# A hybrid state-space and delta-rule decoder layer on one core: prologue scalars and input products moved, the small projection in slots of its own, and the end of the kernel rebuilt with tokens turned before the last norm and six stores

## The chip, the cores and the metric

The kernel runs on one core of a Trainium2 chip. The metric is the device time of one execution in microseconds (us). The kernel before took 2083.59 us, the median of three runs (2082.62 to 2084.09). Engines: PE is TensorE, DVE is VectorE, ACT is ScalarE, POOL is GpSimd, SP is the engine that issues nearly all transfers.

## The reference, cut to what matters

One decoder layer for 320 tokens (256 of a prompt, 8 x 8 of samples) of width 2048, all in float32:

```
h = RMSNorm(x);  proj = h @ w_in -> u | qkv | z | beta | a | gate_s5 | gate_dn
A: S5 state-space model: lambda = exp(a*dt), B' = ((lambda-1)/a) * B, scan over positions, y = Re(C h) + D u
B: gated DeltaNet: beta = sigmoid(.), g = -exp(a_log)*softplus(a + dt_bias), conv + SiLU on q, k, v, chunked delta rule
x = x + (sigmoid(gate_s5)*(A @ w_a) + sigmoid(gate_dn)*(B @ w_b)) @ w_out
x = x + (silu(h2 @ w_gate) * (h2 @ w_up)) @ w_down;  x = x + (p @ w_ple) * sigmoid(h3 @ w_ple_gate)
y = RMSNorm(x) * g_final
```

## The kernel before, in words

Activations lie with features on the partitions: a tile [128, 16, 320] holds x. Weights stream through a ring of four "units"; a unit is 512 KB, four blocks of 128 rows by 256 columns. For every unit SP loads `raw`, ACT copies it to a rounded `whi` (`split_hi`, L909), DVE subtracts to get `wlo` (`split_lo`, L1345), and PE does 24 matmuls of 320 columns (L2035: high times high, high times low, low times high, for two column halves). Units make pairs (four units for a depth of 2048), whose results lie in `pg`, two sets of PSUM banks used in turn, evacuated by DVE.

Small work is laid between the units by an order written out by hand: `schedule()` gives a list of slots, each a list of side jobs and a number of units. PE does a slot's side jobs and then its units. ACT and DVE do the units of a slot (their split) first and then its side jobs. Side jobs of PE write two other PSUM areas, side_a and side_b, whose fills follow the list of `side_fills()`. Each engine runs its instructions in order, so what waits holds up all behind it.

The prologue. Tokens are turned into xt0 (`x`, L2042), weighted by g into xhi and xlo (`x+`). `s5a` computes the S5 scalars on 32 partitions (DVE L1436 to L1448), `s5b` goes on with two Sin on ACT and sixteen DVE instructions (L1456 to L1471). `s5par` turns them (PE L2111) to the layout sp5, `h0` and `cst` turn states (PE L2118, L2095), `rows` squares each token row for the first norm (ACT L1008), `norm` 0 gives the inverse roots. `bmix` multiplies B by the scalars (`b_discrete`, DVE L1486 to L1491, six instructions for each of two factors) and spreads it (L1496), `bb` and `ct` turn B and C (PE L2127, L2148), `k0` multiplies them (L2139), `cadv` advances C by lambda (DVE L1516 to L1522, twice). `ba` is the small projection for beta and a: PE L2159, a copy by DVE (L1618), a turn (`bat`, PE L2165), and then softplus and sigmoid of the decays, with ACT and DVE answering each other (DVE L1630, L1631; ACT L1057, L1059, L1060; DVE L1633, L1634). POOL builds tables of powers of lambda (`tables`) once s5par is there. Then come sixteen s5 slots, a tail, eight `conv` slots of two units each (DVE L1667: nine multiply-adds per head; ACT: `silu_head` and `first_taps`), and the delta rule, output, feed-forward (two halves) and per-layer-embedding parts, the last three in loops.

`pt` turns the embedding input p (PE L2042 on ptok) between the first and the second pair of the first half's down projection; DVE waits there for it and copies it to pf (L1932).

The end. The last pair's gate goes through ACT's sigmoid, DVE multiplies (L1969) and adds to xt (L1972, one instruction for both 128-row blocks), ACT squares (L917) and weights into xg (L1301), POOL adds the squares to acc (L878, L880), PE sums them over partitions (`norm(3)`, L2059), ACT computes the inverse root by Ln and Exp (L935, L942), PE turns xg back to tokens in six fills of eight transposes (`fin`, L2463), ACT and DVE scale each fill into yo (L1331, L2010) and SP stores y in three transfers (L626). yo holds two blocks of tokens, so the third waits for the first store to land.

Of the kernel before, what the change touches and what calls it, by code (L numbers as in the profile page):

```python
# [17 lines left out]
BF16 = mybir.dt.bfloat16  # L18
# [4 lines left out]
P = 128  # L23
# [64 lines left out]
def side_fills():  # L88
# [28 lines left out]
    order += [("ba"[i % 2], ("emb", i)) for i in range(1, KD // 2)] + [("b", ("norm", 3))]  # L117
    order += [("ab"[j % 2], ("fin", j)) for j in range(6)]
# [18 lines left out]
def schedule():  # L137
# [17 lines left out]
    slot([("x", 2), ("x", 3), ("x+", 2), ("x+", 3)], 1)  # L155
# [12 lines left out]
    slot([("pads",)], 1)  # L168
# [5 lines left out]
    for h in range(H):  # L174
        slot([("conv", h)], 2)
# [57 lines left out]
def hybrid_layer(nc, x_prompt, x_sample, state_conv, state_delta, state_s5_re, state_s5_im, p_prompt, p_sample,  # L233
# [25 lines left out]
    with ExitStack() as ctx:  # L259
# [98 lines left out]
        sqj = Zone(nc, ct_end - 5120, 4096).take("sqj", [P, D], BF16)  # L358
# [81 lines left out]
        yo = zo.take("yo", [P, 2, D])  # L440
        xg = zo.take("xg", [P, KD, N])
# [62 lines left out]
        def _(sp):  # L504
# [116 lines left out]
            for t in range(3):  # L621
                dst, n = [(y_prompt[0, 0:P], P), (y_prompt[0, P:2 * P], P),
                          (y_sample.rearrange("b l d -> (b l) d"), NSM)][t]
                for f in (2 * t, 2 * t + 1):
                    wait_drained(sp, ("fin", f))
                sp.dma_start(dst, yo[0:n, t % 2, :]).then_inc(sem(f"y_stored_{t % 2}"), 16)  # L626
            sp.wait_ge(sem("y_stored_0"), 32)
            sp.wait_ge(sem("y_stored_1"), 16)
# [6 lines left out]
        def _(pool):  # L635
# [261 lines left out]
            add_loop(24, 32)  # L897
# [3 lines left out]
        def _(act):  # L901
# [25 lines left out]
            def root(n):  # L927
# [3 lines left out]
                if n == 0:  # L931
                    o.step(act.activation(invt[:, 0:2], ss[:, 0:2], ACT.Ln, scale=1.0 / D, bias=cst[:, 0:1]))
                    o.step(act.activation(invt[0:NSM, 2:3], ss[0:NSM, 2:3], ACT.Ln, scale=1.0 / D, bias=cst[0:NSM, 0:1]))
                elif n == 3:
                    o.step(act.activation(invt[:, 0:2], ps(key)[:, 1, 0:2], ACT.Ln, scale=1.0 / D, bias=cst[:, 0:1]))  # L935
                    drain(act.activation(invt[0:NSM, 2:3], ps(key)[0:NSM, 1, 2:3], ACT.Ln, scale=1.0 / D, bias=cst[0:NSM, 0:1]), key)
                if n < 3:
                    drain(act.activation(inv[:], ps(key)[:, 0, 0:N], ACT.Ln, scale=1.0 / D, bias=cst[:, 0:1]), key)
                wait_drained(act, key)
                o.settle()  # L940
                if n in (0, 3):
                    o.step(act.activation(invt[:, 0:2], invt[:, 0:2], ACT.Exp, scale=-0.5))  # L942
                    act.activation(invt[0:NSM, 2:3], invt[0:NSM, 2:3], ACT.Exp, scale=-0.5).then_inc(sem("invt_ready"), 1)
                if n < 3:
                    act.activation(inv[:], inv[:], ACT.Exp, scale=-0.5).then_inc(sem("inv_ready"), 1)
# [41 lines left out]
            def side(key):  # L987
# [65 lines left out]
                elif what == "ba":  # L1053
# [243 lines left out]
            def final_x(i):  # L1297
                act.wait_ge(sem("xf_ready"), i + 1)
                finish(xt, i + 24, i, None)
# [25 lines left out]
            for t in range(3):  # L1325
                n = CHUNKS[t][1]
                key = ("fin", 2 * t)
                wait_filled(act, key)
                if t == 2:
                    act.wait_ge(sem("y_stored_0"), 16)  # L1330
                drain(act.activation(yo[0:n, t % 2, 0:D // 2].rearrange("p (k c) -> p k c", k=2), ps(key)[0:n], ACT.Copy,  # L1331
                                     scale=invt[0:n, t:t + 1]), key)
# [3 lines left out]
        def _(dve):  # L1336
# [136 lines left out]
            def b_discrete(j):  # L1473

                dve.wait_ge(sem("bnat_landed"), 32)
# [17 lines left out]
                def spread(src, j):  # L1493
                    for r in range(2):
# [999 lines left out]
```

## Time and profile before

| what | value |
|---|---|
| median of three runs | 2083.59 us (2082.62 to 2084.09) |
| profiled execution, its own time | 2082.91 us |
| its span, first to last instruction | 2081.2 us |
| busy: PE, DVE, ACT, POOL | 98%, 54%, 40%, 14% |
| mean granted TensorE clock | 0.990 of full |

The profile is of one execution. A row of the timeline gives the start, the duration, the engine, the line, the operation, its tiles and shapes, and how often it is repeated; a bracket at its end gives the engine's idle time before it and who ended that. A row of the chain of waits gives the start, the duration and what was on the path. Neighbouring PE rows overlap by up to 0.16 us, because matmuls are pipelined.

### The profile page before, as it was taken

How to read it: one execution, taken by the hardware profiler on the slowest of the kernel's cores; microseconds unless marked ns; L12 is line 12 of the kernel's file. 1: busy time of each engine (PE TensorE's matmuls, PEld its weight loads, DVE VectorE, ACT ScalarE, POOL GpSimd, SP SyncE). 2: the span in 40 equal slices, each digit the busy share in tenths (PEclk: the TensorE clock that was granted, in tenths of full speed). 3: DMA queues.
4: the chain of work that ended last, by engine and by line, in shares of the span. 5: the costliest groups of instructions: out<-in, count | busy, mean ns of one | idle time of the engine just before them, and what ended most of it. 6: DMA issues, size and time to landing. Idle time of an engine off the chain costs nothing.

```text
span 2081.2 us, 38416 instructions
## 1 busy us (share of the span) xinstructions
PE 2031.5 (98%) x15445; PEld 1985.8 (95%) x15445; DVE 1125.2 (54%) x1376; ACT 825.7 (40%) x1075; POOL 289.2 (14%) x370
## 2 busy tenths in 40 slices
PE   8899999999999999999999999999999999999997
PEld 7799999988999979999999999999999999999997
DVE  3899896754544477654444444333444444444553
ACT  5343335762323345244433333223333333334543
POOL 2845542000001110011000000000000000011111
PEclk8999999999999999999999999999999999999999
DMA  6544444543334667754444444444544444444442
GB/s 168 162 143 142 131 122 139 154 118 105 96 112 137 176 192 236 235 184 150 152 145 149 151 151 153 131 152 148 158 147 148 151 151 148 140 151 156 143 147 86
DMA packets 299271, 310.13 MB, mean 149 GB/s; under 512 B 24722, under 2 KB 290019, under 8 KB 298531
## 3 DMA queue, kind: packets, MB, share of 16 engines
q1 hardware_dynamic: 295476, 296.76, 46.6%
q0 software_dynamic: 3264, 11.64, 2.1%
q8 instruction: 83, 1.36, 0.3%
q14 instruction: 30, 0.25, 0.0%
q10 hardware_dynamic: 418, 0.12, 0.0%
HBM read 291.34 MB, written 17.14 MB: 148 GB/s over the span
## 4 chain that ended last, share of the span: by engine, by line
PE 88%; DVE 7%; ACT 2%; issue 2%; DMA 1%; SPq 0%; DVEq 0%; ACTq 0%
PE pg L2035 80%; DVE wlo L1345 2%; DVE cacc L1667 2%; PE side_a L2075 1%; PE side_a L2066 1%; ACT whi L909 1%; PE side_b L2075 1%; DMA raw<-in_w_out 0%; PE side_a L2035 0%; PE side_a L2337 0%; DMA xtok<-in_x_sample 0%; PE side_a L2356 0%; PE side_b L2298 0%; PE side_b L2035 0%; PE side_a L2314 0%
## 5 line engine op out<-in xcount | busy, mean ns | idle before, releaser
L1345 DVE TENSOR_TENSOR wlo<-raw,whi 128x1024 fp32r<-128x1024 f32 (+1 forms) x528 | 650.1, 1239 | 699.0 <-ACT whi L909 697.3
L909 ACT ACTIVATE whi<-raw 128x1024 fp32r<-128x1024 f32 (+1 forms) x528 | 544.8, 1039 | 910.7 <-PE pg L2035 872.2
L2035 PE MATMUL pg<-xhi,whi 128*128 128x320 f32 x2816 | 882.8, 313 | 15.9 <-DVE wlo L1345 15.6
L2035 PE MATMUL pg<-xlo,whi 128*128 128x320 f32 x2816 | 872.5, 310 | 0.0
L2035 PE MATMUL pg<-xhi,wlo 128*128 128x320 f32 x2816 | 872.5, 310 | 0.0
L2035 PEld LDWEIGHTS pg<-xhi,whi 128*128 128x128 f32 x2816 | 531.1, 189 | 25.1 <-issue 13.7
L2035 PEld LDWEIGHTS pg<-xlo,whi 128*128 128x128 f32 x2816 | 531.4, 189 | 0.8
L2035 PEld LDWEIGHTS pg<-xhi,wlo 128*128 128x128 f32 x2816 | 531.0, 189 | 0.0
L2035 PE MATMUL pg<-mhi,whi 128*128 128x320 f32 x704 | 217.4, 309 | 2.5 <-DVE wlo L1345 2.5
L2035 PE MATMUL pg<-mlo,whi 128*128 128x320 f32 x704 | 217.4, 309 | 0.0
L2035 PE MATMUL pg<-mhi,wlo 128*128 128x320 f32 x704 | 217.4, 309 | 0.0
L893 POOL TENSOR_TENSOR fsi<-fsg,inv 128x640 f32<-128x640 f32 x22 | 43.4, 1971 | 710.0 <-ACT fsg L1240 710.0
L2035 PEld LDWEIGHTS pg<-mhi,whi 128*128 128x128 f32 x704 | 132.2, 188 | 2.6 <-issue 2.6
L2035 PEld LDWEIGHTS pg<-mhi,wlo 128*128 128x128 f32 x704 | 132.2, 188 | 0.0
L2035 PEld LDWEIGHTS pg<-mlo,whi 128*128 128x128 f32 x704 | 132.2, 188 | 0.0
L639 POOL TENSOR_TENSOR pt<-ta,tb 128x256 f32<-128x256 f32 x64 | 72.5, 1151 | 99.7 <-DVE gg L1568 98.4
L878 POOL TENSOR_TENSOR acc<-acc,sq 128x320 f32<-128x320 f32 x24 | 24.2, 1007 | 411.6 <-ACT sq L917 411.6
L2035 PE MATMUL pg<-mxhi,whi 128*128 128x320 f32 x256 | 79.2, 309 | 0.4 <-DVE wlo L1345 0.4
L2035 PE MATMUL pg<-mxlo,whi 128*128 128x320 f32 x256 | 79.1, 309 | 0.0
L2035 PE MATMUL pg<-mxhi,wlo 128*128 128x320 f32 x256 | 78.7, 308 | 0.0
L2035 PEld LDWEIGHTS pg<-mxhi,whi 128*128 128x128 f32 x256 | 48.1, 188 | 0.6 <-issue 0.6
L2035 PEld LDWEIGHTS pg<-mxlo,whi 128*128 128x128 f32 x256 | 48.0, 188 | 0.0
(460 smaller groups left out, 1954.1 us busy)
## 6 DMA issues: line engine op xcount, KB each, us to landing
raw<-in_w_in SPq DMA_DIRECT2D x144, 512.0 KB, 3.8
raw<-in_w_gate SPq DMA_DIRECT2D x88, 512.0 KB, 3.5
raw<-in_w_up SPq DMA_DIRECT2D x88, 512.0 KB, 3.5
raw<-in_w_down SPq DMA_DIRECT2D x80, 512.0 KB, 3.5
raw<-in_w_out SPq DMA_DIRECT2D x32, 512.0 KB, 3.5
raw<-in_w_ple_gate SPq DMA_DIRECT2D x32, 512.0 KB, 3.5
raw<-in_w_a SPq DMA_DIRECT2D x16, 512.0 KB, 5.4
raw<-in_w_b SPq DMA_DIRECT2D x16, 512.0 KB, 4.3
```

What stands on the lines that cost most here:

```text
L639: ins = pool.tensor_tensor(out, a, b, op)
L878: pool.tensor_tensor(acc[:], acc[:], sq[:, 0, :], ALU.add).then_inc(sem("pool_steps"), 1)
L893: pool.tensor_tensor(fsi[:], fsg[:], inv[:].unsqueeze(1).broadcast_to([P, 2, N]), ALU.mult).then_inc(sem("fsi_ready"), 1)
L909: act.activation(whi[:, r, 0:nk, :], raw[:, r, 0:nk, :], ACT.Copy).then_inc(w_hi, 1)
L1345: dve.tensor_tensor(wlo[:, r, 0:nk, :], raw[:, r, 0:nk, :], whi[:, r, 0:nk, :].bitcast(F32), ALU.subtract).then_inc(w_lo, 1)
L1667: ins = dve.scalar_tensor_tensor(out=s, in0=qkv[:, t, j:j + NCV], scalar=w, in1=s, op0=ALU.mult, op1=ALU.add)
L2035: ins = pe.matmul(out[:, m, 0:N], w, a, start=first and k == 0 and part == 0, stop=last and k == nk - 1 and part == 2)
L2066: ins = pe.matmul(out[0:rows or P, h // 4, (h % 4) * n:(h % 4) * n + n], lhs(h), rhs(h), start=True, stop=True)
L2075: ins = pe.matmul(out[r, h // 4, (h % 4) * HB:(h % 4 + 1) * HB], lhs(h, r), rhs(h, r), start=True, stop=True)
```

## The change

- `slots`: `s5a` and `s5b` stand one slot earlier and ahead of the x jobs; the products of `bmix` are a job `bprod` of their own, in the slots of rows 0 (factor 1) and rows 1 (factor 0); `bmix` keeps the spread, both in one slot; `cadv` 0 has a slot to itself; `bat` is split from `ba` and stands in the slot of `pads`; the decays (`decay` 0 and 1) move to the conv slots of heads 4 and 5. The number of units in all these slots together is unchanged.
- The squares' scratch sqj lies elsewhere, since the products now use its old place.
- `pt` moves from the first half's down projection to behind the first gate pair of the second half.
- The last squares (block pair 7): DVE's addition to xt is cut in two, ACT squares each, and DVE adds each to acc (POOL did). A square root with a reciprocal on DVE takes the place of Ln and Exp; a tiny Sqrt stands ahead of the last squares.
- `fin`: the first halves of tokens 0 to 127 and 128 to 255 are turned ahead of norm(3), the second into pg; the other two are turned after it; the samples' two halves are made by sixteen matmuls into 128 partitions and scaled by one instruction into their own tile yo2. Six stores of half the columns replace three.

```diff
-    slot([("x", 4), ("x", 5), ("x+", 4), ("x+", 5), ("s5a",)], 1)
-    slot([("x", 6), ("x", 7), ("x+", 6), ("x+", 7), ("s5b",)], 1)
-    slot([("s5par",), ("h0",), ("cst",), ("rows", 0)], 1)
-    slot([("rows", 1)], 1)
+    slot([("s5a",), ("x", 2), ("x", 3), ("x+", 2), ("x+", 3)], 1)
+    slot([("s5b",), ("x", 4), ("x", 5), ("x+", 4), ("x+", 5)], 1)
+    slot([("x", 6), ("x", 7), ("x+", 6), ("x+", 7)], 1)
+    slot([("s5par",), ("h0",), ("cst",), ("rows", 0), ("bprod", 1)], 1)
+    slot([("rows", 1), ("bprod", 0)], 1)
...
-    slot([("bmix", 1)], 2)
-    slot([("bmix", 0)], 1)
+    slot([("bmix", 1), ("bmix", 0)], 2)
     slot([("bb", 1), ("ct",)], 1)
-    slot([("bb", 0), ("k0",), ("cadv", 0)], 1)
+    slot([("bb", 0), ("k0",)], 1)
+    slot([("cadv", 0)], 1)
     slot([("cadv", 1)], 1)
     slot([("ba",)], 1)
-    slot([("pads",)], 1)
+    slot([("bat",), ("pads",)], 1)
...
-        slot([("conv", h)], 2)
+        slot([("conv", h)] + [("decay", h - 4)] * (4 <= h < 6), 2)
...
-                elif what == "ba":
+                elif what == "decay" and a[0] == 0:
                     act.wait_ge(sem("gab_landed"), 32)
                     o.step(act.activation(gab[:, 0:H], gab[:, 0:H], ACT.Exp))
                     act.wait_ge(sem("ba_vector"), 1)
...
+                if c == 1:
+                    wait_filled(dve, ("pt",))
+                    drain(dve.tensor_copy(pf[:], ps(("pt",))[:, :, 0:N]), ("pt",))
+                    wait_drained(dve, ("pt",))
...
+            o.step(act.activation(dl[:, 0:1], cst[:, 0:1], ACT.Sqrt))
             final_x(7)
-            root(3)
+            key = ("norm", 3)
+            wait_filled(act, key)
+            drain(act.activation(invt[:, 0:3], ps(key)[:, 1, 0:3], ACT.Sqrt, scale=1.0 / D, bias=cst[:, 0:1]), key)
...
+            dve.wait_ge(sem("acc_added"), 31)
+            for m in range(2):
+                dve.wait_ge(sem("last_squares"), m + 1)
+                dve.tensor_tensor(acc[:], acc[:], sq[:, m, :], ALU.add).then_inc(sem("last_added"), 1)
+                dve.wait_ge(sem("last_added"), m + 1)
+            wait_drained(dve, ("norm", 3))
+            dve.reciprocal(invt[:, 0:3], invt[:, 0:3]).then_inc(sem("invt_ready"), 1)
...
+            pe.wait_ge(sem("xg_ready"), 8)
+            end(turned(begin(("fin", 0, 0)), 0, 0), ("fin", 0, 0))
+            pe.wait_ge(evacuated, PLE_P + 7)
+            turned(pg[:, 0], 1, 0).then_inc(sem("turned_0"), 1)
+            norm(3)
             pe.wait_ge(sem("xg_ready"), KD)
-            norm(3)
...
+            pe.wait_ge(evacuated, PLE_P + 8)
+            turned(pg[:, 1], 0, 1).then_inc(sem("turned_1"), 1)
+            end(turned(begin(("fin", 1, 1)), 1, 1), ("fin", 1, 1))
+            out = begin(("fin", 2))
+            for k in range(8):
+                for half in range(2):
+                    ins = pe.matmul(out[NSM * half:NSM * half + NSM, k // 4, (k % 4) * P:(k % 4 + 1) * P],
+                                    xg[:, 8 * half + k, NPR:N], ident[:], start=True, stop=True)
+            end(ins, ("fin", 2))
```

## Rows read from the trace of the kernel before

**Rows 1.** The page: busy time of the engines, and the chain's shares by engine
```profile
PE 2031.5 (98%) x15445; PEld 1985.8 (95%) x15445; DVE 1125.2 (54%) x1376; ACT 825.7 (40%) x1075; POOL 289.2 (14%) x370
...
PE 88%; DVE 7%; ACT 2%; issue 2%; DMA 1%; SPq 0%; DVEq 0%; ACTq 0%
```

**Rows 2.** Stretches: length, busy time and instructions per engine, PE clock, DMA share, GB/s
```profile
90.00:100.00 10.00, 7.32 (x56) 5.73 (x56) 9.79 (x11) 0.00 (x0) 9.54 (x9) 0.83 0.19 54
...
160.00:200.00 40.00, 40.00 (x384) 38.62 (x383) 38.42 (x64) 14.82 (x25) 22.82 (x23) 1.00 0.47 138
```

**Rows 3.** A wait of PE from 0 to 130 us: total, times, longest
```profile
PE side_a L2111 <- DVE sc L1471: 4.3, 1, 4.3
```

**Rows 4.** The chain of waits from 24 to 112 us
```profile
34.55 0.28 DVE sc L1456
...
38.90 0.95 PE side_a L2111 x7
...
40.90 2.70 PE side_a L2095 x24
...
44.16 1.99 ACT sqj L1008 x2
...
61.23 0.64 DVE bt L1486
...
84.43 0.83 DVE ctl L1516
...
98.17 1.58 DVE wlo L1345
...
100.44 0.85 PE side_a L2165 x6
...
102.37 0.22 ACT sp L1057
...
105.66 1.05 ACT whi L909
...
108.01 4.09 PE pg L2035 x26
```

**Rows 5.** Matmuls of L2035 alone in two stretches: PE and PEld busy, clock
```profile
43.51:49.02 5.51, 5.51 (x26) 5.51 (x27) 0.65 0.02 6
...
53.29:67.60 14.31, 14.31 (x96) 14.07 (x96) 1.00 1.06 289
```

**Rows 6.** PE alone in two stretches: bb 1 to k0, and the first s5 drive
```profile
104.93:106.30 1.37, 1.37 (x33) 1.00 0.00 0
72.56:84.39 11.83, 10.65 (x203) 1.00 0.32 95
```

**Rows 7.** Timeline of ACT and DVE in the conv slots of heads 4 and 5
```profile
372.44 1.99 ACT L909 ACTIVATE whi<-raw 128x1024 fp32r<-128x1024 f32 x2
...
372.41 4.72 DVE L1667 SCALAR_TENSOR_TENSOR cacc<-qkv,par,cacc 128x344 f32<-128x344 f32 x9
377.05 1.22 DVE L1345 TENSOR_TENSOR wlo<-raw,whi 128x1024 fp32r<-128x1024 f32 x1
```

**Rows 8.** Timeline of PE behind the turns of p
```profile
1332.56 0.38 PE L2035 MATMUL pg<-mhi,whi 128*128 128x320 f32 x1 [2.46 <-DVE wlo L1345]
```

**Rows 9.** Timeline of the end
```profile
2061.15 0.82 DVE L1972 TENSOR_TENSOR xt<-xt,fmd 128x640 f32<-128x640 f32 x1
...
2064.80 1.28 PE L2059 MATMUL side_b<-ones,acc 128*128 128x1 f32 x6 [4.54 <-issue]
...
2069.48 1.91 PE L2463 MATMUL side_a<-ident,xg 128*128 128x128 f32 x8
...
2076.52 0.54 SPq L626 DMA_DIRECT2D out_y_sample<-yo  x1
```

**Rows 10.** The chain of waits at the end
```profile
2069.82 1.29 DVE yo L2010
2071.18 3.90 DMA out_y_prompt<-yo
```

More of the change, by code:

```diff
@@ L116, in side_fills @@
     order += [("a", ("norm", 1)), ("b", ("pt",)), ("a", ("emb", 0)), ("b", ("norm", 2))]
-    order += [("ba"[i % 2], ("emb", i)) for i in range(1, KD // 2)] + [("b", ("norm", 3))]
-    order += [("ab"[j % 2], ("fin", j)) for j in range(6)]
+    order += [("ba"[i % 2], ("emb", i)) for i in range(1, KD // 2)]
+    order += [("b", ("fin", 0, 0)), ("a", ("norm", 3)), ("a", ("fin", 1, 1)), ("b", ("fin", 2))]
     count, signals, at = {"a": 0, "b": 0}, {"a": 0, "b": 0}, {}
@@ L440, in hybrid_layer @@
         yo = zo.take("yo", [P, 2, D])
+        yo2 = zo.take("yo2", [P, D // 2])
         xg = zo.take("xg", [P, KD, N])
@@ L618, in _ @@
                                   rows_of(w, k0, nk, bass.ds((it * 4 + b) * PW, PW)), nk)
[L621 to L628, printed above, removed]
+            first, second = slice(0, D // 2), slice(D // 2, D)
+            wait_drained(sp, ("fin", 0, 0))
+            sp.dma_start(y_prompt[0, 0:P, first], yo[:, 0, first]).then_inc(sem("y_stored"), 16)
+            sp.wait_ge(sem("y_scaled_0"), 1)
+            sp.dma_start(y_prompt[0, P:2 * P, first], yo[:, 1, first]).then_inc(sem("y_stored"), 16)
+            sp.wait_ge(sem("y_scaled_1"), 1)
+            sp.dma_start(y_prompt[0, 0:P, second], yo[:, 0, second]).then_inc(sem("y_stored"), 16)
+            wait_drained(sp, ("fin", 1, 1))
+            sp.dma_start(y_prompt[0, P:2 * P, second], yo[:, 1, second]).then_inc(sem("y_stored"), 16)
+            wait_drained(sp, ("fin", 2))
+            for k, cols in enumerate((first, second)):
+                sp.dma_start(y_sample.rearrange("b l d -> (b l) d")[:, cols], yo2[NSM * k:NSM * k + NSM, :]).then_inc(sem("y_stored"), 16)
+            sp.wait_ge(sem("y_stored"), 16 * 6)
             sp.wait_ge(sem("tail_stored"), 32)
@@ L1626, in side @@
                     wait_drained(dve, key)
+                elif what == "decay" and a[0] == 0:
                     dve.wait_ge(sem("gab_landed"), 32)
@@ L1970, in ple_out @@
                 wait_drained(dve, key)
-                xs = xt[:, 2 * i:2 * i + 2, :]
-                dve.tensor_tensor(xs, xs, fmd[:], ALU.add).then_inc(sem("xf_ready"), 1)
-                dve.wait_ge(sem("xf_ready"), i + 1)
+                if i < 7:
+                    xs = xt[:, 2 * i:2 * i + 2, :]
+                    dve.tensor_tensor(xs, xs, fmd[:], ALU.add).then_inc(sem("xf_ready"), 1)
+                    dve.wait_ge(sem("xf_ready"), i + 1)
+                else:
+                    for m in range(2):
+                        dve.tensor_tensor(xt[:, 14 + m, :], xt[:, 14 + m, :], fmd[:, m, :], ALU.add).then_inc(sem("xf_ready"), 1)
             dve.wait_ge(sem("phi_ready"), 1)
@@ L2058, in norm @@
                     for c, (c0, n) in enumerate(CHUNKS):
-                        ins = pe.matmul(out[0:n, 1, c:c + 1], acc[:, c0:c0 + n], ones[:, 0:1], start=True, stop=True)
+                        for r in range(0, P, n):
+                            ins = pe.matmul(out[r:r + n, 1, c:c + 1], acc[:, c0:c0 + n], ones[:, 0:1], start=True, stop=True)
                 end(ins, key)
@@ L2160, in side @@
                     end(ins, key)
-                    wait_drained(pe, key)
-                    key = ("bat",)
+                elif what == "bat":
+                    wait_drained(pe, ("ba",))
                     out = begin(key)
@@ L2422, in _ @@
                     norm(1)
+                else:
+                    pe.wait_ge(sem("p_landed"), 48)
+                    key = ("pt",)
+                    out = begin(key)
+                    for m in range(2):
+                        ins = token_transposes(out[:, m], slice(m * P, (m + 1) * P), ptok)
+                    end(ins, key)
                 gate_up(0, 1)
@@ L2430, in _ @@
                 down(0, 0, lambda j: pe.wait_ge(sem("mlo_ready"), c * (KFC // 2) + min(2 * (j + 1), KFC // 2)))
-                if c == 0:
-                    pe.wait_ge(sem("p_landed"), 48)
-                    key = ("pt",)
-                    out = begin(key)
-                    for m in range(2):
-                        ins = token_transposes(out[:, m], slice(m * P, (m + 1) * P), ptok)
-                    end(ins, key)
                 down(0, 1)
```

104 lines of the change are left out of this document (53 added, 51 removed).

## The prediction, made before the change was run

> **What bounds the kernel now.** I read the page first, then the stretches, then the chain of waits at both ends and the timelines there. The page says PE: busy 98% of the span, 88% of the chain [rows 1]. In the middle nothing else counts: from 160 to 200 us PE is busy 40.0 of 40.0 us and DVE, at 38.4, still keeps up [rows 2]. So a change of side work pays only where PE stands still. It does in four places. (1) At 34.6 us PE waits 4.3 us for the sixteen small DVE instructions of `s5b` [rows 3, 4], and its clock is then low: the unit at 43.51 takes 5.51 us at a granted 0.65, where four units at full clock take 14.31, 3.5 each [rows 5]. (2) From 61 to 107 us the chain is nearly all DVE: products, spreads, cadv, the decays [rows 4]; between 90 and 100 us PE works 7.3 of 10 us [rows 2]. (3) Behind the turns of p, PE stands 2.46 us [rows 8]. (4) At the end everything is a chain. The reader should also see in rows 7 that the conv slots have no such slack on DVE: nine multiply-adds end at 377.05 and the next wlo starts in that moment.
>
> **The prologue: -10.** I follow the new order with the old durations. The old unit 2 begins at 30.85, a microsecond after its transposes are over, because `s5a` stands ahead of its split; with s5a and s5b earlier, DVE has both behind it by 26, and unit 2 begins at 29.8 and ends at 33.3. s5par's turn starts there and not at 38.90, and cst ends at 38.0 and not at 43.6 (4.7 us of turns either way) [rows 4]. Unit 3 runs from 38.0.
>
> ACT then has cst's copy, rows 0 (old start 44.16, now 38.6), whi 4 until 41.4, rows 1 and 2 until 45.3, whi 5 and 6 until 47.3. DVE was idle here. It now does product 1 from 35.3 to 39.5 (six of 0.64 to 0.7, 4.2 us [rows 4]), wlo 4 behind whi 4 until 42.6, product 0 until 47.0, wlo 5 until 48.2. These 8.7 us of products leave the stretch in which DVE is the bound. Their price: PE gets unit 4 only at 42.6 and unit 5 only at 48.2, two gaps of about 1.1 us each. (The rows job took 2.0 with its read [rows 4], a whi 1.0 [rows 7].) Unit 5 began at 53.3, so it is 5.1 us early. Units 5 to 8 are PE's own (14.1 us [rows 5]) and end at 62.3; the root of the norm (ready at 51.4), the splits of 7 and 8, both spreads and wlo 9 end on DVE at 60.9, hidden. The stretch bb 1, ct, one unit, bb 0, k0 took 11.83 us, 0.5 of it waiting for wlo [rows 6]; it now follows unit 8 and holds unit 9 (before, unit 9 came ahead of it and unit 10 was in it): 62.3 to 73.5, with unit 10 right behind, 73.5 to 77.0, and unit 11 to 80.5. From k0's end on DVE bounds as before: k0's copy, whi 11 and wlo 11 (the old order had wlo 11 done already: +2.8), then cadv 0, wlo 12, cadv 1, wlo 13, 84.43 to 99.75 or 15.3 us [rows 4], so 76.3 to 91.6. PE stands 3.5 us ahead of unit 12 and 1.7 ahead of unit 13, as it did 4.2 before.
>
> Then the decays are gone. Before, 8.3 us lay between wlo 13 (99.75) and unit 14 (108.01): bat, two DVE instructions, 3.3 us in which ACT has Exp, a table load, Ln, a table load and Sigmoid (102.37 to 105.66), whi, wlo [rows 4]. Now: unit 13 (3.5), bat (0.85 [rows 4]), the first drive (1.4 [rows 6]), 5.7 us. Unit 14 starts at 97.3 and not 108.0: -10.7. From there PE is the bound and DVE has more room than before.
>
> The clock: PE has only turns from 33.3 to 38.0 and small gaps after, so units 3 and 4 may still run low. Two units at 5.5 and not 3.5 would take the place of the 1.1 us gaps and push unit 5 by about 0.7. I take that: -10.0; bounds -7 (the low clock lasts over four more units, 1.5 to 2 us each, partly in gaps) and -12 (no low clock, DVE's shares of 1.24 to 1.63 us per wlo at the short end).
>
> The Trainium skill, "TensorE: Matmul & The Clock Gate", section "Part 4: PE-mode transpose", says that transposes don't count as PE-busy for the clock. The trace leans that way at the end: behind the norm PE has nothing but turns, and the third eight of them still take 1.91 us [rows 9]. By that rule alone the stretch 33.3 to 38.0 is as good as idle, and the low clock would come back a few us earlier than in the old kernel; rival (b) is what it would do then.
>
> Queues that the moved steps pass: SP's order is the same; its loads wait for w_lo, which comes earlier, and the four cnat loads follow load 9 at about 49 and are needed at 64.5. POOL's tables start with s5par, 5 us earlier, and were done with the first phases (92) long before DVE wants them (101 now). The spar values had landed before DVE wants them at 16.3. Moving sqj costs nothing: same ACT instructions.
>
> **p's turns: -2.5.** The idle 2.46 us [rows 8] comes because DVE waits for the turn with the next units' split queued behind it. In the new place DVE has just done gate_out of the very pair that PE turns behind; wlo of the next pair's first three units is done, and the next whi comes 3 us later. Turn (1.1 us) and copy (0.8) are paid in both. Bounds 0 and -2.6.
>
> **The decays in conv slots 4 and 5: +5.3.** This is the edit that I expect to cost. ACT's `decay` 0 waits for DVE's two instructions, which stand behind conv 4 (old end 377.05 [rows 7]). Queued behind ACT's wait are whi of the next two units, which before were made at 372.44, and DVE's next instruction needs the first of them. So: conv 4 ends 377.05; the two DVE instructions 0.4; ACT's Exp, load, Ln, load, Sigmoid 3.3 [rows 4]; whi 1.05 [rows 4]; wlo at 381.9 and not 377.05. Its unit started about 1.5 us after the old wlo began, with no finished unit queued in front, so PE stands 4.4 us. `decay` 1 adds 0.4 in a stage in which DVE has no idle time at all, and some of decay 0's 0.4 is in the 4.8 already: 4.8 + 0.4 = 5.2, and 0.1 to 0.4 for a clock that falls after such a gap (unit 12 behind the 4.2 us gap had 0.83 in its slice [rows 2]). Value 5.3, bounds 4 and 6.5; 0 if ACT's wait is somehow over before. ACT's later load for SiLU (1.3) is ahead of need. So a third of the gain of the prologue comes back as a loss, and the 3.3 us of ACT that were on the path there are on the path here.
>
> The Trainium skill, "ScalarE: Activation LUTs", section "What ACT_TABLE_LOAD costs", gives 2.66 us for each switch, load and drain; the trace has 3.3 us for two loads and three activations together [rows 4], so the drain isn't seen. By the page this step would be +8 (estimate).
>
> **The end: -4.2.** Old: xt's addition 2061.15, norm(3) at 2064.80 for 1.28, then until 2069.82 for the roots and the second fill, stores at 2071.18 and later, the third one at 2076.52, held up by the landing of the first (3.90 us) [rows 9, 10]. New: the first half of the addition ends at 2061.6 (half of 0.82), square 2062.15, DVE's two additions 2062.65 and 2063.2: norm(3) at 2063.25, 1.5 early. Eight matmul rows, not six: 1.4 (+0.1). Sqrt 0.3, no second table load (1.28 saved; the first is taken by the tiny Sqrt, under DVE's multiply and add), reciprocal 0.25: roots at 2065.3 and not 2068.1. ACT and DVE scale at once, first stores at 2066.6. The turns after the norm: at the low clock 1.7 per eight [rows 9], 2068.1. The samples: sixteen float32 matmuls. No row has this form; below, half the columns of two column groups at once at full clock, 1.8 us; above, 32 passes one by one at low clock, 6.8. I take 3.5 (low clock, two at once), as the eight turns before them are low: 2071.6. Scaling 1.2, stores at 2072.9 and 2073.4, landing 3.5 (between the old 3.90 and less for a fourth of the size), and the rest of the old end (0.45): 2077. Old 2081.2: -4.2; bounds -2 and -7.2. Six issues of about 0.54 [rows 9] lie in SP's idle time but for the last one.
>
> **Sum.** -10.0 - 2.5 + 5.3 - 4.2 = -11.4 on the span of 2081.2; the profiled execution took 1.7 more than its span, and the median of the runs is 0.7 over the execution. 2083.6 - 11.4 = 2072.2.
>
> **Rivals.** (a) The decays cost nothing: -5.3 more, 2067. For it: ACT is idle over half of the conv stage. Against: the order of ACT's queue. Chance 0.12. (b) The low clock, 1.2 of 2.4 GHz, comes back with the turns at 33 to 38 and holds into units 5 and 6: two units at 5.3 and not 3.5, +3.5, 2075.7. For it: the old clock fell behind the same turns and stayed low into unit 3 [rows 5]. Against: there 4.3 us of idling came first [rows 3]. Chance 0.17. (The Trainium skill's page on TensorE, quoted above, would have this one.) (c) The lead of the prologue is given back in the s5 slots, if DVE (38.4 of 40 us [rows 2]) and not PE sets their pace: 10 us back, 2082. Against it: PE has no gap there. Chance 0.05. (d) Slower: the clock stays low from unit 3 to k0 and beyond. A unit costs up to 3.5 more at half clock; units 5 to 10 are six, 21 us, so 2093. It decides from the fourth low unit on. Against it: units 5 to 8 ran at 1.00 right behind a low stretch [rows 5]. Chance 0.02. (e) The end alone is not what it says (samples' matmuls one by one): +3.3, 2075.5, within my range; 0.1. My forecast has 0.54.
>
> **Numbers.** 2072.2; the terms' bounds together give 2064 to 2078 in practice, since they won't all fall on one side: range 2065 to 2079. What a measurement can tell from no change is about 0.2%, 4.2 us: faster means under 2079.4. All but (c) and (d) are: 0.91 faster, 0.06 within, 0.03 slower.
>
> **What would show it.** s5par's turn at 33 to 34 us; unit 14 near 97; DVE idle some 4.5 us after the fifth conv, with ACT's Exp, Ln, Sigmoid there and PE waiting 4.4 us for wlo near 368 (all is 10 us earlier); no gap behind p's turns; norm(3) 3 us after the last sigmoid's end; the last store issued some 13 us after it. I am wrong if the clock is low past 50 us, or if that PE gap near 368 isn't there.

## The result, and the profile after

The changed kernel takes 2066.86 us (median of 4 runs, 2066.31 to 2068.49), the kernel before 2083.23 us (median of 4 in the same comparison): ratio 0.992, 95% interval 0.9907 to 0.9933. That is 16.4 us less, where 11.4 less were forecast (2072.2, range 2065 to 2079). The profiled execution took 2068.49 us with a span of 2066.8, against 2082.91 and 2081.2 before: 14.4 us of span, which the traces divide as follows.

| part | forecast | traces |
|---|---|---|
| prologue, to the start of unit 14 | -10.0 | -11.5 (108.01 to 96.48) |
| decays in the conv slots | +5.3 | +5.8 |
| p's turns | -2.5 | -2.5 |
| the end | -4.2 | -6.2 |
| sum on the span | -11.4 | -14.4 |

The other 2 us between 14.4 and 16.4 lie in the executions: the profiled one is the slowest of four. Another execution of the same kernel (e8 below) has a span of 2064.5; where it gained is shown there. Below, PE's clock is called full where 1.00 was granted and low where 0.50 was (1.2 of 2.4 GHz); a unit with a granted mean between the two was low for a part of its time.

The page after answers to [rows 1]. PE has 4.8 us less busy time, and its share of the chain has gone from 88% to 91%: there is less waiting for others on it.

```profile
PE 2026.7 (98%) x15463; PEld 1983.0 (96%) x15463; DVE 1124.4 (54%) x1379; ACT 827.3 (40%) x1075; POOL 288.2 (14%) x368
...
PE 91%; DVE 5%; ACT 2%; issue 1%; DMA 1%; SPq 0%; ACTq 0%; DVEq 0%
```

The chain from 24 to 112 us (start, us, what), beside [rows 4]: s5par's turn at 34.02 and not 38.90, the product (L1500, for `bnat`) between two units, cadv at 75 and not 84, and unit 14 at 96.55 with no ACT chain ahead of it.

```profile
34.02 0.55 PE side_a L2143 x7
...
37.34 1.99 ACT sqj L1009 x2
...
41.57 0.69 DVE bnat L1500
...
47.04 14.35 PE pg L2064 x96
...
75.05 0.66 DVE ctl L1530
...
96.55 15.60 PE pg L2064 x105
```

Unit 3 in the stretch table (length, PE busy, clock, DMA share, GB/s), beside the unit of 5.51 us at 0.65 in [rows 5]: full clock. The next row is the unit behind the wait for cadv 0, the third the unit behind the new stall in the conv slots.

```profile
36.68:40.46 3.78, 3.78 (x24) 1.00 0.40 133
82.04:87.33 5.29, 5.29 (x24) 0.68 0.35 102
371.56:377.42 5.86, 5.86 (x26) 0.60 0.74 200
```

The new stall, beside [rows 7]: the timelines of ACT, DVE and PE. ACT's second Exp (L1058) waits 3.44 us for DVE's L1649, which stands behind the conv; the two splits (L915) come at 369.21; DVE idles 4.40 us for them, PE 4.34.

```profile
365.70 0.18 DVE L1649 SCALAR_TENSOR_TENSOR sp<-ba 128x24 f32<-128x24 f32 x1
365.92 0.22 ACT L1058 ACTIVATE sp<-sp 128x24 f32<-128x24 f32 x1 [3.44 <-DVE sp L1649]
366.16 1.28 ACT L1060 ACT_TABLE_LOAD   x1
367.46 0.31 ACT L1060 ACTIVATE sp<-sp,ones 128x24 f32<-128x24 f32 x1
367.79 1.28 ACT L1061 ACT_TABLE_LOAD   x1
...
369.21 1.99 ACT L915 ACTIVATE whi<-raw 128x1024 fp32r<-128x1024 f32 x2
370.29 1.23 DVE L1358 TENSOR_TENSOR wlo<-raw,whi 128x1024 fp32r<-128x1024 f32 x1 [4.40 <-ACT whi L915]
371.56 0.63 PE L2064 MATMUL pg<-xhi,whi 128*128 128x320 f32 x1 [4.34 <-DVE wlo L1358]
```

PE's waits from 830 to 1400 us: where [rows 8] had 2.46 us behind the turns of p, the longest is 0.5.

```profile
PE pg L2064 <- DVE wlo L1358: 0.5, 1, 0.5
```

The end, beside [rows 9]: the turns of the first prompt half at 2051.89 (L2491), ahead of the norm; norm(3) 2.25 us after the last addition begins (before 3.65); all turns of eight at 1.03 to 1.09 us, not 1.91; the samples' 32 passes in 1.97.

```profile
2051.89 1.03 PE L2491 MATMUL side_b<-ident,xg 128*128 128x128 f32 x8
...
2052.94 0.90 DVE L1995 TENSOR_TENSOR xt<-xt,fmd 128x320 f32<-128x320 f32 x2
...
2055.19 0.82 PE L2091 MATMUL side_a<-ones,acc 128*128 128x1 f32 x8 [1.40 <-DVE acc L2028]
2055.94 1.09 PE L2491 MATMUL pg<-ident,xg 128*128 128x128 f32 x8
...
2057.77 0.36 SPq L624 DMA_DIRECT2D out_y_prompt<-yo  x1
2057.84 1.97 PE L2505 MATMUL side_b<-ident,xg 128*64 128x128 f32 x32
...
2060.99 2.28 SPq L633 DMA_DIRECT2D out_y_sample<-yo  x2
```

### The profile page after: what moved, and what is told of

Same layout as the page of the kernel before. It is cut to its first block, busy times and chain, and to the rows that moved or that the text cites. A ratio compares the mean times of both kernels' runs of the same rounds, so it can differ in the third digit from the quotient of the medians.

```text
span 2066.8 us, 38448 instructions
## 1 busy us (share of the span) xinstructions
PE 2026.7 (98%) x15463; PEld 1983.0 (96%) x15463; DVE 1124.4 (54%) x1379; ACT 827.3 (40%) x1075; POOL 288.2 (14%) x368
## 4 chain that ended last, share of the span: by engine, by line
PE 91%; DVE 5%; ACT 2%; issue 1%; DMA 1%; SPq 0%; ACTq 0%; DVEq 0%
PE pg L2064 83%; DVE wlo L1358 2%; PE side_a L2107 1%; DVE cacc L1687 1%; PE side_a L2098 1%; ACT whi L915 1%; PE side_b L2107 1%; DMA raw<-in_w_out 0%; PE side_a L2369 0%; PE side_a L2064 0%; DMA xtok<-in_x_sample 0%; PE side_a L2388 0%; PE side_b L2330 0%; PE side_b L2064 0%; PE side_a L2346 0%
## 5 line engine op out<-in xcount | busy, mean ns | idle before, releaser
L915 ACT ACTIVATE whi<-raw 128x1024 fp32r<-128x1024 f32 (+1 forms) x528 | 545.1, 1040 | 922.2 <-PE pg L2064 887.9
L2064 PE MATMUL pg<-xhi,whi 128*128 128x320 f32 x2816 | 883.2, 314 | 16.4 <-DVE wlo L1358 16.2
```

What stands on the lines that cost most here:

```text
L915: act.activation(whi[:, r, 0:nk, :], raw[:, r, 0:nk, :], ACT.Copy).then_inc(w_hi, 1)
L2064: ins = pe.matmul(out[:, m, 0:N], w, a, start=first and k == 0 and part == 0, stop=last and k == nk - 1 and part == 2)
```

## The experiments

All were timed beside the kernel before, in three groups of four, in which it had medians of 2083.32 (e1 to e4), 2083.89 (e5 to e8) and 2083.45 (e9 to e12). "Against changed" takes the changed kernel's distance to before as 16.4, which both its comparisons gave (2083.23 - 2066.86, and 2083.89 - 2067.57 = 16.3). The intervals reach some 3 us to either side (2 for e4, e5 and e9). Among the variants of the changed kernel only e6's stands clear of the changed kernel's own. No single time of e2, e3, e7, e11 or e12 lies within its 2066.3 to 2068.5, but those of e1 come up to it (2066.29) and those of e10 lie partly in it: what e1 and e10 are worth is read from places in the traces.

| run | us | ratio to before, 95% | against changed |
|---|---|---|---|
| e1 decays back in slot 14 | 2065.86 | 0.9914 (0.9900, 0.9927) | -1.1 |
| e2 DVE's part a slot ahead | 2063.40 | 0.9902 (0.9887, 0.9917) | -3.5 |
| e3, e12 decays cut up by table | 2062.25, 2061.19 | 0.9895 (0.9880, 0.9910) | -4.7, -5.9 |
| e4 before + s5a, s5b early | 2077.62 | 0.9973 (0.9962, 0.9984) | |
| e5 before + the new end | 2077.93 | 0.9971 (0.9960, 0.9982) | |
| e6 products back | 2074.41 | 0.9957 (0.9944, 0.9971) | +6.9 |
| e7 early turns behind the norm | 2070.25 | 0.9936 (0.9922, 0.9949) | +2.8 |
| e8 changed kernel again | 2067.57 | 0.9924 (0.9911, 0.9938) | |
| e9 before + p's turns | 2080.60 | 0.9986 (0.9977, 0.9995) | |
| e10 row sums later | 2065.83 | 0.9919 (0.9906, 0.9933) | -1.2 |
| e11 cut up, row sums later | 2061.25 | 0.9893 (0.9878, 0.9909) | -5.8 |

**e1, decays back in slot 14.**

```
-    slot([("bat",), ("pads",)], 1)
+    slot([("bat",), ("decay", 0), ("decay", 1), ("pads",)], 1)
-        slot([("conv", h)] + [("decay", h - 4)] * (4 <= h < 6), 2)
+        slot([("conv", h)], 2)
```

> The changed kernel with both parts of the decays back in slot 14, all else as changed. My theory: the stall of PE behind the fifth conv (gap of 4.34 us, low clock behind it; 5.8 us by the shift of the units) is gone. In the prologue the decays cost less than the 5.8 us that they cost in the conv slots, because wlo of unit 14 and the first drive can stand around ACT's chain of 3.3 us: unit 14 starts 1.5 to 2.5 us later than 96.5. Sum -3.3 to -4.3 us, about 2063. Rival: the chain DVE, ACT, DVE is on the path in both places and costs the same wherever it stands, 5 to 6 us: unit 14 starts at 102, and the time stays at 2067 within 1 us.

The stall in the conv slots is gone, and unit 14 starts at 96.34, no later than with the change. But the unit behind it waits 1.88 us for its wlo and runs at 0.68 of the clock. Timeline of PE, then its stretches for unit 14 and the next:

```profile
102.00 0.41 PE L2064 MATMUL pg<-xhi,whi 128*128 128x320 f32 x1 [1.88 <-DVE wlo L1358]
```

```profile
96.34:100.12 3.78, 3.78 (x24) 1.00 0.02 4
102.00:107.32 5.32, 5.32 (x26) 0.68 0.77 221
```

Counted by the start of the same unit (329.9 in e1, 326.4 changed) the decays cost 3.5 us here, and 5.8 in the conv slots, by the changed kernel's shift against the kernel before; behind both places e1 is 2.2 ahead (412.1 and 414.3), and 1.1 in the medians. Both theories missed: unit 14 covers part of ACT's chain, as mine had it, but not most, and it costs 3.5 where I had 1.5 to 2.5 and the rival 5 to 6.

**e2, DVE's part one slot ahead of ACT's.** ACT's five instructions stay where they are.

```
-        slot([("conv", h)] + [("decay", h - 4)] * (4 <= h < 6), 2)
+        slot([("conv", h)] + [("decay", h - 3)] * (3 <= h < 6), 2)
-                elif what == "decay" and a[0] == 0:     # ACT's five
+                elif what == "decay" and a[0] == 1:
-                elif what == "decay":                   # DVE's last two
+                elif what == "decay" and a[0] == 2:
```

> The changed kernel, the decays still in the conv slots, but DVE's first two instructions one slot ahead of ACT's five (slots of heads 3 and 4), and DVE's last two one slot behind them. So ACT waits for nothing. My theory: the loss comes from ACT's wait for the end of DVE's fifth conv, with whi of the next two units queued behind it. Without the wait ACT's five instructions (Exp, Exp, Ln, Sigmoid and the table loads, about 4.8 us) run beside DVE's conv of 4.7 us, and whi comes 1 us late instead of 5: PE's gap there is 1 to 2 us and not 4.3, sum -3.5 to -4.5 us, about 2063. Rival: the table loads and five activations in ACT's queue are the cost, whatever they wait for: the gap stays at 3 us or more, sum -1.3 or less, 2065.5 to 2067.

Timelines of ACT and DVE: the second Exp (L1058) waits for nothing, the splits start 3.3 us behind it, and DVE waits 0.96 us and not 4.40.

```profile
361.77 0.21 ACT L1058 ACTIVATE sp<-sp 128x24 f32<-128x24 f32 x1
...
365.05 2.00 ACT L915 ACTIVATE whi<-raw 128x1024 fp32r<-128x1024 f32 x2
...
366.20 1.23 DVE L1358 TENSOR_TENSOR wlo<-raw,whi 128x1024 fp32r<-128x1024 f32 x1 [0.96 <-ACT whi L915]
```

PE's waits there are 2.1 us in four pieces, none over 0.7. The same instructions on the same engine in the same slot: what cost was the wait, not the work. -3.5, at the edge of what I expected.

**e3, decays cut up by activation table.** A piece stands only where its table is loaded anyway.

```
+    slot([("bat",), ("decay", 0), ("pads",)], 1)                 # Exp twice, DVE's first two
+        slot([("decay", 1)] * (h == 7) + [("conv", h)], 2)       # Sigmoid
+        slot([("l2", j)] + ... + [("decay", j + 2)] * (j in (0, 2)), 1)   # Ln; DVE's last two
```

> The changed kernel with the decays cut up by activation table, each piece where its table is loaded anyway: both Exp and DVE's first two instructions in slot 14, Sigmoid ahead of the conv side in the slot of head 7, Ln in the first l2 slot, DVE's last two in the third. My theory: no piece makes ACT wait and none needs a load of its own, so the whole 5.8 us come back less some tenths: 2061 to 2061.8, with PE's gap behind the fifth conv gone and unit 14 at 96.5 to 97.3. Rival: small waits of ACT for DVE in slot 14 (Exp behind DVE's two additions) push the first drives, and the l2 slots have no room: unit 14 at 98.5 or a gap in l2, 2063 to 2064.

PE's waits from 340 to 380 us are those of the kernel before again (0.7 us in three pieces):

```profile
PE pg L2066 <- DVE wlo L1360: 0.7, 3, 0.2
```

Unit 14 starts at 94.8 (95.5 in e12), so slot 14 isn't pushed. 4.7 and 5.9 us less than the changed kernel in two comparisons, around the 5.8 of the stall. This is the version that beats both kernels: 2061.2 to 2062.3.

**e4, the kernel before with s5a and s5b early, alone.**

```
-    slot([("x", 2), ("x", 3), ("x+", 2), ("x+", 3)], 1)
-    slot([("x", 4), ("x", 5), ("x+", 4), ("x+", 5), ("s5a",)], 1)
-    slot([("x", 6), ("x", 7), ("x+", 6), ("x+", 7), ("s5b",)], 1)
+    slot([("s5a",), ("x", 2), ("x", 3), ("x+", 2), ("x+", 3)], 1)
+    slot([("s5b",), ("x", 4), ("x", 5), ("x+", 4), ("x+", 5)], 1)
+    slot([("x", 6), ("x", 7), ("x+", 6), ("x+", 7)], 1)
```

> The kernel before with one edit: s5a and s5b each one slot earlier and ahead of the slot's splits; products, decays, turns and end as before. My theory: PE's wait of 4.3 us at 34.6 goes, and with it the low clock of unit 3 (2 us), so unit 5 starts about 6 us earlier (47 to 48). But from 61 to 107 DVE is the bound with its two products still there, so only what DVE gets earlier counts: its products start when the spreads' rows are there, 5 to 6 us earlier, and unit 14 starts 4 to 6 us earlier: 2077.5 to 2079.5. Rival: the products set the time of that stretch by themselves (8.7 us of DVE behind rows that come from ACT), and the early start is worth under 2 us without their move: 2081.5 or more.

-5.7 us, unit 14 at 102.3 and not 108.0: my theory. Its timeline of PE ahead of units 4 and 5 also shows what I had not asked: the gaps that I had put down to the products are there without them (1.24 and 0.75 in the changed kernel).

```profile
41.90 0.41 PE L2035 MATMUL pg<-xhi,whi 128*128 128x320 f32 x1 [1.13 <-DVE wlo L1345]
46.99 0.42 PE L2035 MATMUL pg<-xhi,whi 128*128 128x320 f32 x1 [0.50 <-DVE wlo L1345]
```

**e5, the kernel before with the new end, alone.** The diff is the part of the change from `norm(3)` on.

> The kernel before with the new end alone (first prompt half's turns ahead of the last norm, Sqrt in place of Ln and Exp, xt's last addition and the squares in two halves, samples' turns as matmuls in two column groups, six stores). My theory after the trace of the changed kernel, where norm(3) to the last instruction took 11.6 us and 16.4 before: the end is worth 6.2 us by itself, 2077.1 (2076.4 to 2077.8), two thirds of it ahead of the stores; at full clock in the turns. Rival: the old prologue leaves the low clock at the end (as in the kernel before), the eight turns behind the norm and the samples then take up to twice their 1.1 and 2.0 us, and it is worth 3.5 to 4.5 us: 2079 to 2079.8.

-6.0. Here the clock did fall behind the norm (it was low from 2066.6 to 2070.0), and it cost nothing. Timeline of the end:

```profile
2064.97 0.82 PE L2086 MATMUL side_a<-ones,acc 128*128 128x1 f32 x8 [1.40 <-DVE acc L2023]
...
2066.71 1.91 PE L2486 MATMUL side_a<-ident,xg 128*128 128x128 f32 x8
...
2068.56 2.64 PE L2500 MATMUL side_b<-ident,xg 128*64 128x128 f32 x32
...
2072.39 1.18 SPq L633 DMA_DIRECT2D out_y_sample<-yo  x2
```

The last stores are issued 7.4 us after the norm's start and not 5.8, but the span ends 11.6 us after it in both (2076.5 - 2065.0, 2066.8 - 2055.2). Why is answered by e7.

**e6, the products back ahead of the spreads.**

```
-    slot([("s5par",), ("h0",), ("cst",), ("rows", 0), ("bprod", 1)], 1)
-    slot([("rows", 1), ("bprod", 0)], 1)
+    slot([("s5par",), ("h0",), ("cst",), ("rows", 0)], 1)
+    slot([("rows", 1)], 1)
-    slot([("bmix", 1), ("bmix", 0)], 2)
+    slot([("bprod", 1), ("bmix", 1), ("bprod", 0), ("bmix", 0)], 2)
```

> The changed kernel with the two input products back directly ahead of their spreads (DVE 8.7 us), s5a and s5b left where the change put them. My theory: the two small gaps of 1.24 and 0.75 us ahead of units 4 and 5 close to 1.1 and 0.5 or less, but from 60 us the 8.7 us are on the path again; some of it is DVE's slack there, and unit 14 starts 4.5 to 6.5 us later than 96.5: 2071.5 to 2073.5. Rival: s5a and s5b did it all, and the products stand where DVE would have been idle anyway: unit 14 within 1.5 us of 96.5, 2067 to 2068.5.

+6.9: my theory, a little over its range. PE stands 3.82 us where it stood 0, and the unit behind runs low (5.24 us). The small gaps go back to e4's 1.13 and 0.50: the products' price in them is 0.36 us together. But the 6.9 is not what moving them away from the old order brought. e6 has both products and both spreads in one slot, which neither kernel has, and its unit 14 starts at 103.3, later than e4's 102.3, though e4 has the decays ahead of it as well. Timeline of PE:

```profile
70.17 0.63 PE L2064 MATMUL pg<-xhi,whi 128*128 128x320 f32 x1 [3.82 <-DVE wlo L1358]
```

**e7, the early turns behind the norm.** `norm(3)` stands ahead of the first prompt half's turns in PE's order; nothing else is changed.

```
+            norm(3)
             pe.wait_ge(sem("xg_ready"), 8)
             end(turned(begin(("fin", 0, 0)), 0, 0), ("fin", 0, 0))
             pe.wait_ge(evacuated, PLE_P + 7)
             turned(pg[:, 0], 1, 0).then_inc(sem("turned_0"), 1)
-            norm(3)
```

> The changed kernel with norm(3) ahead of the first prompt half's turns, as the old order had it; all else of the new end as it is. PE then stands idle for some 3.5 us ahead of the norm, and has eight turns more behind it. My theory: the early turns both save their own 1.8 us and keep PE busy, so that the clock is still full behind the norm; without them the clock falls and turns and samples behind the norm run at half speed: the end is 1.8 + 1.1 + 1 to 2 us longer, +3.5 to +5, 2070.3 to 2072. Rival: the clock has nothing to do with it, only the turns' own time is added: +1.8 or less, up to 2068.7.

+2.7 against e8 in the medians, less than mine and more than the rival; from the norm to the end the traces differ by 1.8, which is the rival's number. Its mechanism isn't there, though: the clock did fall (low from 2056.3 to 2059.7), and sixteen turns took 3.27 us. Timeline:

```profile
2054.93 0.82 PE L2091 MATMUL side_a<-ones,acc 128*128 128x1 f32 x8 [3.15 <-DVE acc L2028]
2055.68 1.44 PE L2491 MATMUL side_b<-ident,xg 128*128 128x128 f32 x8
...
2056.91 3.27 PE L2491 MATMUL pg<-ident,xg 128*128 128x128 f32 x16
...
2064.14 1.17 SPq L633 DMA_DIRECT2D out_y_sample<-yo  x2
```

The last stores are issued 9.2 us after the norm, 3.4 later than in the changed kernel, but only 1.8 of it reach the end, since they land sooner. The DMA view of the end, 2055 to 2067 and 2069 us in 40 slices (tenths of the engines' time, GB/s, and for the samples' stores KB each and the median from issue to landing), the changed kernel first, then e7:

```profile
DMA  0000000000009999999999999999999997970000
GB/s 0 0 0 0 0 0 0 0 0 0 0 0 396 410 382 437 396 369 423 410 382 423 410 410 369 423 423 410 382 314 287 191 205 232 382 273 0 0 0 0
...
out_y_sample<-yo SPq DMA_DIRECT2D x2, 256.0 KB, 4.5
```

```profile
DMA  0000000000009996069999999999579997930000
...
out_y_sample<-yo SPq DMA_DIRECT2D x2, 256.0 KB, 3.1
```

With the change the 16 DMA engines are busy without a break from 2058.6 to 2065.8, 7.2 of the 9.0 us from the first store's issue to the end of the span (a slice is 0.3 us in the first, 0.35 in the second): 2.62 MB, at about 400 GB/s in most slices. The stores are now the bound of the end, and PE's clock behind the norm is covered by them. e5 shows the same. This end isn't always the same length, though: of the ten traces that have it unaltered, eight need 11.5 to 11.6 us from the norm to the end of the span, and e3 and e11 need 12.6 and 12.7. The last stores are issued no later there (5.8 us after the norm) and land later; why is open.

**e8, the changed kernel once more.**

> The changed kernel as it is, on the chip of this group of runs, to compare the other three with: 2066.9 (2066 to 2068). In its profile I look for what differs from execution to execution: the place of the low clock behind the turns of 33 to 37 us and behind the gap at 371 us. My theory: these places are the same in every execution. Rival: the low clock comes or stays away by chance, and with it 1.5 to 3.5 us, which would explain that the decays in slot 14 gained 2.6 us in the profiled execution and 1.0 in the medians.

The low clock behind the waits at 82 and at 370 us is there both times. Near 650 us it is not: PE in the stretch 640 to 660 of the changed kernel's first trace, then of e8. Nothing ahead of it differs by more than 0.3 us, and a shift of 1.5 us between the two appears there; 0.8 more of the 2.3 us between the spans comes between 740 and 880 us.

```profile
640.00:660.00 20.00, 20.00 (x142) 0.91 0.37 106
```

```profile
640.00:660.00 20.00, 20.00 (x152) 1.00 0.41 110
```

PE is busy throughout in both, and e8 is not the usual case: nine of the fourteen traces have a low stretch between 640 and 662 us, and e5 to e9 have none. So both theories hold, each for its places, and a difference of about 2 us between two single traces says nothing before it is placed.

**e9, the turns of p alone.** In the kernel before, `if c == 0` becomes `if c == 1` for p's turns and their copy.

> The kernel before with one edit: the turns of p and their copy behind gate_out of chunk 1 and not chunk 0. My theory: the 2.46 us in which PE waits for wlo behind the turns go whole and nothing else moves, since DVE has done the splits that it needs: -2.5 us on the span, no gap of PE over 0.3 us near 1332, and the shift of the last units against the kernel before is the same 2.5. Rival: the copy of p in its new place pushes the next split, and a gap of 0.5 to 2 us shows behind chunk 1: -0.5 to -2.

-2.9 us (-1.0 to -4.8), and PE has no wait at all in the list from 1250 to 1400 us. My theory.

**e10, row sums later.**

```
-    slot([("s5par",), ("h0",), ("cst",), ("rows", 0), ("bprod", 1)], 1)
-    slot([("rows", 1), ("bprod", 0)], 1)
-    slot([("rows", 2)], 0)
+    slot([("s5par",), ("h0",), ("cst",), ("bprod", 1)], 2)
+    slot([("rows", 0), ("rows", 1), ("rows", 2), ("bprod", 0)], 0)
```

> The changed kernel with ACT's three row sums (2.1 us each) and DVE's second product behind the splits of units 4 and 5, in a slot of no unit of their own. My theory: PE's gaps of 1.24 us ahead of unit 4 and 0.75 us ahead of unit 5 come from ACT, which has a row sum ahead of each whi, and not from the products: they close, everything up to k0's turns comes 1.8 to 2.1 us earlier, and unit 14 too: 2065.0 to 2065.8 beside 2067.2. Rival 1: the products on DVE make the gaps: they stay at 0.7 us or more. Rival 2: the gaps close, but DVE's chain from k0 to unit 13 sets unit 14, and takes back the lead: time within 0.5 us of the changed kernel's.

The gap ahead of unit 4 closes, but ACT's three sums now stand together ahead of the next split, and the gap ahead of unit 5 grows to 1.21 (0.75). k0's turns end 1.2 us earlier, unit 14 starts at 94.25 (96.2 to 96.5). 1.2 us in the medians, whose intervals overlap. This run alone doesn't part the two engines, since product 1 too now stands behind the split of unit 4; and ahead of unit 5 both are late, ACT with its split at 44.2 us and DVE with the products at 44.6. What speaks for ACT is this run together with e4 and e6, which have no product there and gaps of 1.13 and 0.50 us: most of the gaps is ACT's, as in my theory, with half the gain that I had given it. Of the 2.2 us at unit 14, 1.2 come from here. The rest is DVE's own: cadv 0 and the split behind it take 5.8 us (73.78 to 79.56) and in the changed kernel the same instructions 6.8 (74.98 to 81.82). Why is open.

**e11 and e12, both together, and e3 again.** e11 has the edits of e3 and e10; e12 is e3's kernel.

> Both improvements together: decays cut up by activation table, and row sums behind the splits of units 4 and 5. Theory: they lie in different stages and add, 4.7 and 2 us under the changed kernel: 2059.9 to 2060.8. Rival: the shift by 2 us leads to more low clock in one of the places where it comes by chance (near 650 and 750 us), and no more than 1 us of the second is seen: 2061.5 or more.

> The kernel with the decays cut up by activation table once more, to compare with on this chip, 2061.5 to 2063. In its profile I look at the stretch behind the turns of 33 to 37 us, where the first execution had a low clock of 3.4 us and the changed kernel none in two executions. Theory: it comes there by chance, with no idle time ahead of it, and costs under 0.5 us since ACT has PE wait there anyway. Rival: it belongs to this kernel and is there again.

e11's gain over e12 is none (2061.25, 2061.19). My sum was wrong, and the rival has the right kind of reason in another place. PE's stretches of units 12 and 13, e11 and then e12:

```profile
79.89:83.64 3.75, 3.75 (x24) 1.00 0.52 144
87.78:93.10 5.32, 5.32 (x24) 0.68 0.71 197
```

```profile
81.08:86.37 5.29, 5.29 (x24) 0.68 0.36 102
88.96:92.75 3.79, 3.79 (x24) 1.00 0.59 161
```

e12 has the low clock in unit 12, where PE afterwards waits for cadv 1 on DVE anyway, and it costs nothing. e11 starts unit 12 1.2 us earlier, waits 1.85 us ahead of unit 13, and has the low clock in that unit, which is on the path: 1.5 us, and the lead is gone. e10, with the same order up to here, had neither unit low, so it is not the order alone. For e12's other question: PE from 30 to 45 us in e3, then e12.

```profile
30.00:45.00 15.00, 15.00 (x109) 0.89 0.45 136
```

```profile
30.00:45.00 15.00, 13.77 (x109) 1.00 0.47 145
```

The same kernel, once low and once not, with the same 109 matmuls in both: the low unit, right behind the turns (32.7 to 35.5 us), fills the gap in which PE waits for ACT's row sum. What sets it off is open; it isn't the kernel, and it costs nothing here (unit 14 at 94.8 with it, 95.5 without).

## Why the prediction was right, and where it missed

The measured 2066.86 lies 5.3 us from the forecast value and 1.9 inside its range. It is also the number that rival (a) had (2067, the decays cost nothing), and that rival is false: they cost 5.8 us. The time alone could not tell the two apart; the traces do. Of the 5.0 us between 16.4 and 11.4, 3.0 are terms of the sum (prologue 1.5 and end 2.0 in one direction, decays 0.5 in the other) and 2.0 are the difference between the profiled executions and the medians. One step of the range was added up wrongly: the terms' bounds (-12, -2.6, +4, -7.2 and -7, 0, +6.5, -2) give -17.8 to -2.5, or 2065.8 to 2081.1, and not 2064 to 2078. The measured time lies in either.

**The prologue, -10.0 against -11.5.** The order of events was right: cst's turns end at 36.75 (38.0 forecast), unit 5 starts at 47.04 (48.2), cadv 0 at 75.05 (76.3), unit 14 at 96.48 (97.3). The step that missed is the clock: units 3 and 4 were to run low (0.7), and the turns were to take 4.7 us "either way". With no idle ahead of them they took 2.8 at full clock. The 11.5 come apart along a row of kernels, each of which makes one more step in the prologue. The split of the same unit starts at 141.6 us in the kernel before, at 135.8 in e4 (s5a and s5b: 5.7), at 133.5 in e1 (products, spreads and slots too: 2.3) and at 130.0 in the changed kernel (decays out: 3.5). The 8.7 us of DVE's products, the largest move of the plan, thus brought the least of the three in this order; e6's 6.9 for them holds for another arrangement of the slots. The products' price was put too high and on the wrong engine: two gaps of 1.1 us, of which e4 has 1.6 in all without any product; most of them is ACT's row sums (e4, e6, e10).

**Rival (b), the low clock behind turns,** did not happen in either trace of the changed kernel. Of the eleven traces in which s5a and s5b are early, ten have full clock from 30 to 45 us with 2.8 us of nothing but turns in it; e3 is low from 36.4 to 39.8, behind the turns. The prediction argued for this rival that the old clock fell behind the same turns. It fell ahead of them: it was low from 37.1 us in the kernel before, in PE's wait of 4.3 us, and from 36.5 in e9 (wait 4.3) and 39.1 in e5 (wait 2.7), where the turns start at 38.90, 38.68 and 39.52. In e5 it had been low before, from 32.2 to 35.6, with PE busy. So which idle time is enough to lose the clock isn't shown, but turns alone didn't lose it in ten of eleven cases, and they don't keep it from coming back. PE in two stretches of the kernel before, 24 turns in each:

```profile
2066.01:2071.40 5.39, 5.39 (x26) 0.50 0.00 0
2071.50:2074.80 3.30, 2.99 (x24) 1.00 0.87 355
```

In e7 too the clock is full again from 2059.7, when PE had done only turns since 2055.7. The Trainium skill, "TensorE: Matmul & The Clock Gate", section "Part 4: PE-mode transpose", says of the transpose mode that it doesn't count as PE-busy in the same way. The traces go against it as a rule for these turns, in the prologue and at the end: the prediction's "the trace leans that way" rested on the third eight of them (1.91 us) and left out the fourth and fifth, at 1.19 and 1.06.

**Rivals (c) and (d)** did not happen. The same unit is 11.6 us early at 130 us and 11.6 at 290, so the s5 slots give nothing back, and the clock is full from 21 to 82 us.

**The decays, +5.3 against +5.8.** Every step is in the trace: the wait for L1649 behind the conv, Exp to Sigmoid in 3.4 us, splits queued behind, DVE's wait of 4.40, PE's of 4.34 (4.4 forecast). What was too small is the clock behind it: the unit took 5.86 us and not 3.7, of which DVE's backlog hides some; I had 0.1 to 0.4 for it. e2 shows the mechanism, by taking away the wait and leaving ACT's five instructions where they are. Each table load takes 1.28 us, and its activation starts 0.01 to 0.02 us after it. The Trainium skill, "ScalarE: Activation LUTs", section "What ACT_TABLE_LOAD costs", has 2.66 us for each switch. This trace agrees with its 1.28 for the load and shows no drain, and the step isn't the +8 that I had estimated from the page.

**p's turns, -2.5 against -2.5,** alone too (e9).

**The end, -4.2 against -6.2 (e5: -6.0).** The norm came 1.4 us early, as forecast (1.5). The failed step is PE's durations behind it, all taken at the low clock: 1.4 for the norm's eight rows (0.82 in both traces), 1.7 for eight turns (1.09 and 1.04), 3.5 for the samples (1.97). The early turns stand in PE's former idle time of 4.54 us, and the clock was full until the samples were done. In e5 it fell just ahead of the second eight turns (2066.6, they start at 2066.71) and the samples took 2.64, still well under 3.5, and the span ended at the same distance from the norm. So the rest of the clock's effect is covered by what the forecast had not as a bound at all: the stores' own traffic, which fills the DMA engines for 7.2 of the 9.0 us from the first issue to the end of the span (2057.77 to 2066.8).

The misses of the prologue and of the end are of one kind: where PE's idle time goes, its low clock mostly goes too, and I counted the first and not the second.

## What to carry to other kernels

Before moving small activations into a slot with "idle" ACT time, look at what stands ahead of the wait on the other engine and what is queued behind it on ACT: here 0.4 us of DVE work behind a conv of 4.7 us held up two weight splits, and PE for 4.3 us; put the producer a slot ahead, or cut the group up by activation table. When a wait of PE goes, take the low clock behind it out of the sum as well, but count a low unit only where PE doesn't wait for someone else right after it. At an end with stores, find out from which moment on the DMA engines are full; work behind that moment is hidden.

## What the runs showed of the hardware that I had not expected

- 32 float32 passes of 128 columns on 64 output partitions, in two column groups, took 1.97 us at full clock; eight turns of 128 columns on 128 partitions took 1.04. The two groups ran at once: the passes start in pairs 0.006 us apart, and a pair follows the last by 0.10 to 0.11, as one turn follows another.
- The low clock has places where it returns (behind the waits at 82 and 370 us in both traces of the changed kernel) and others where it comes and goes with nothing in the kernel changed: near 650 us (nine of fourteen traces; in the changed kernel's first, PE had no wait over 0.21 us from 600 us on), and between 30 and 45 us in one of the eleven with s5a and s5b early.
- The clock came back to full while PE did nothing but turns: at 2071.5 us in the kernel before, at 2059.7 in e7.
- SP's issue of a store took 0.36 us for the first and 2.28 for the last two together in the changed kernel, and 1.17 for the same two in e7, where the DMA engines had been less full.
